# The group norm of an RWKV layer, as a stage of its own or inside the trips of the scan

## The reference, cut to what matters

```python
    _, y = lax.scan(step, S0, (tm(r_h), tm(w_h), tm(k_h), tm(v_h), tm(kk), tm(a_h)))
    y = tm(y)
    mean = jnp.mean(y, axis=-1, keepdims=True)
    var = jnp.mean(jnp.square(y - mean), axis=-1, keepdims=True)
    y = ((y - mean) * lax.rsqrt(var + RW_GN_EPS) * ln_w.reshape(RW_HEADS, RW_HEAD)
         + ln_b.reshape(RW_HEADS, RW_HEAD))
    y = y + jnp.sum(r_h * k_h * r_k, axis=-1, keepdims=True) * v_h
    y = y.reshape(B, T, D) * gate
    return y.astype(h.dtype) @ w_out
```

## Time and profile before

| | us |
|---|---|
| median of three runs | 3041.53 |
| the profiled execution, its own time | 3047.19 |
| span of its trace | 3045.4 |
| scan, from its first DMA issue to the last state update | 514.2 to 955.5 |
| gn, from its first instruction to the next stage's first | 956.5 to 1045.0 |
| PE busy over the span | 2654.7 (87%) |
| DVE, ACT, POOL busy over the span | 884.6, 548.9, 218.2 |
| granted TensorE clock, mean | 0.945 of 2.4 GHz |

### The profile page before, as it was taken

How to read it: one execution, slowest core, us unless ns; L and a number is a source line. 1 busy time by engine, 2 the same in 40 slices (tenths; PEclk the granted TensorE clock), 3 DMA queues, 4 the chain that set the end, 5 groups by cost and what they waited for, 6 DMA issues and landing times. The chain is left out here.

```text
span 3045.4 us, 44485 instructions
## 1 busy us (share of the span) xinstructions
PE 2654.7 (87%) x18608; PEld 1421.0 (47%) x18608; DVE 884.6 (29%) x1598; ACT 548.9 (18%) x892; POOL 218.2 (7%) x209
## 2 busy tenths in 40 slices
PE   5798996989887695999999969999669869999993
PEld 2243442888885253444443434444544534444441
DVE  6233001666565534111110122000762431101013
ACT  3342000223233311000000011300451100000000
POOL 0000000001010400001010000000010010100100
PEclk9999998999998897999999989999889979999997
DMA  3242133131323523799999940221433259999995
GB/s 117 112 143 99 62 103 97 45 82 48 82 49 151 212 118 140 259 413 410 411 407 399 392 152 38 94 79 55 118 130 136 95 196 377 417 413 417 413 404 225
DMA packets 264767, 617.51 MB, mean 203 GB/s; under 512 B 37377, under 2 KB 128658, under 8 KB 262546
## 3 DMA queue, kind: packets, MB, share of 16 engines
q1 hardware_dynamic: 233362, 524.72, 46.3%
q10 hardware_dynamic: 17408, 56.63, 4.7%
q0 software_dynamic: 13824, 33.58, 2.8%
HBM read 545.67 MB, written 85.98 MB: 207 GB/s over the span
## 5 line engine op out<-in xcount | busy, mean ns | idle before, releaser
L1812 PE MATMUL moe_first_psum<-moe_ring,moe_first_x_t 128*64 128x512 f32 (+1 forms) x1504 | 508.9, 599 | 7.3 <-DMA moe_ring<-in_moe_w_in 3.7
L560 PE MATMUL proj_psum<-proj_mix,proj_ring 128*128 128x512 f32 x768 | 337.1, 599 | 15.9 <-ACTq L72 10.1
L1812 PEld LDWEIGHTS moe_first_psum<-moe_ring,moe_first_x_t 128*64 128x64 f32 (+1 forms) x1504 | 198.1, 165 | 280.0 <-issue 275.2
L1812 PE MATMUL moe_first_psum<-moe_ring,moe_first_act_t 128*128 128x512 f32 (+1 forms) x800 | 282.1, 594 | 0.0
L1408 PE MATMUL moe_route_psum<-moe_ring,trunk_mixed 128*128 128x512 f32 x512 | 230.3, 605 | 22.8 <-PEq L106 22.8
L560 PEld LDWEIGHTS proj_psum<-proj_mix,proj_ring 128*128 128x128 f32 x768 | 147.1, 193 | 200.4 <-issue 188.7
L1853 DVE TENSOR_TENSOR moe_first_act<-moe_first_silu,moe_first_psum 128x512 f32<-128x512 f32 x48 | 33.0, 688 | 688.6 <-ACT moe_first_silu L1869 688.6
L2146 PE MATMUL hproj_psum<-trunk_mixed,moe_ring 128*128 128x512 f32 x512 | 220.0, 592 | 1.8 <-ACTq L72 1.8
L1812 PE MATMUL moe_first_psum<-trunk_mixed,moe_first_x_t 128*128 128x512 f32 (+1 forms) x544 | 196.1, 593 | 0.0
L1812 PEld LDWEIGHTS moe_first_psum<-moe_ring,moe_first_act_t 128*128 128x128 f32 (+1 forms) x800 | 105.8, 162 | 131.5 <-issue 131.5
L1408 PEld LDWEIGHTS moe_route_psum<-moe_ring,trunk_mixed 128*128 128x128 f32 x512 | 96.9, 194 | 137.2 <-issue 137.2
(11 more groups left out here) (339 smaller groups left out, 3075.2 us busy)
## 6 DMA issues: line engine op xcount, KB each, us to landing
moe_ring<-in_moe_w_in SPq DMA_DIRECT2D x94, 2048.0 KB, 18.0
moe_ring<-in_moe_w_out SPq DMA_DIRECT2D x50, 2048.0 KB, 19.9
trunk_mixed<-in_moe_w_in SPq DMA_DIRECT2D x34, 2048.0 KB, 20.3
trunk_mixed<-in_moe_w_out SPq DMA_DIRECT2D x14, 2048.0 KB, 21.1
moe_ring<-expert_rows SPq DMA_DIRECT2D x16, 1024.0 KB, 7.9
proj_ring<-in_rw_in SPq DMA_DIRECT2D x12, 1024.0 KB, 6.1
moe_ring<-gate_cm SPq DMA_DIRECT2D x16, 512.0 KB, 4.4
normed_rows<-moe_x SPq DMA_DIRECT2D x16, 512.0 KB, 2.6
```

Of the source, the lines that this page charges most:

```text
L560: mm = pe.matmul(psum[:, bank + half, :], ring[slot][:, k, part * P:(part + 1) * P], src[:, k, half * HALF:(half + 1) * HALF], start=(k == ...
L1812: mm = t.matmul(e.psum[rows, bank + a, :], left[:, k0 + k, rows], weights.units[m % RING][:, k, a * HALF:(a + 1) * HALF], start=(part != " ...
```

## The change

1. **Means, in proj.** Where DVE copied the turned v tile, it now sums each head (a reduce of 1024 columns to 16) and writes v minus the mean as `v_rows`. `v_cm`, read for the bonus, stays as it was. y comes out of the scan with mean zero.
2. **Norm of the trip before, in the scan.** `GroupNorm` (new) works on a tile of 128 tokens, all channels. In trip t ACT squares y of trip t-1 at the start of b = 0; PE sums the squares after step 1 (two products of 512 columns); ACT takes logarithms after step 2 and the inverse root after step 3; POOL multiplies (four pieces of 256 columns); ACT applies weight and bias at the start of b = 1 (eight of 128 columns); POOL adds the bonus and multiplies by the gate (eight pieces).
3. **Bonus of this trip.** POOL multiplies r and k from the tiles that the scan holds (four pieces); PE sums them over heads with eight matrices `rk_ones` after step 1 of b = 1 (eight products of 128 columns); DVE multiplies v with the sums after step 3 of b = 1 (two of 512 columns, and eight small ones before the scan to make `rk_ones`).
4. **Loads.** SP loads a v tile and a gate tile per trip (512 KB each) and, at the start of the scan, the 4 MB of `w_out`. r and k are not loaded again.
5. **Loops.** `all_trips` is written out on every engine.
6. **The last tile's norm goes into moe0_route**: ACT squares, PE sums ahead of the first product, ACT inverts, POOL multiplies behind its tables, ACT applies weight and bias after the first tile's scaling, POOL finishes; PE waits for that ahead of its eighth tile. SP waits for it ahead of loading unit 5, whose memory the norm uses.
7. **The stage gn is gone.** Three units of the weight ring (`late`) live through the whole trunk so that the norm and `w_out` have a place; in the HGRN2 scan three tiles move into it. The routing and mixture code is otherwise the same.

```diff
@@ rwkv_project, vector
-                    v.tensor_copy(mix[0][:, b, :], psum[:, 4 + 2 * b:6 + 2 * b, :].rearrange("p a t -> p (a t)")
-                                  ).then_inc(v_dve.sem, 1)
+                    v.wait_ge(v_dve.sem, v_dve.after("copy", tile - 1))
+                    rows_p = psum[:, 4 + 2 * b:6 + 2 * b, :].rearrange("p a (n e) -> p (a n) e", e=HEAD)
+                    v.tensor_reduce(head_total[:], rows_p, AX_X, ALU.add).then_inc(v_dve.sem, 1)
...
+                    v.scalar_tensor_tensor(out=mix[0][:, b, :].rearrange("p (n e) -> p n e", e=HEAD),
+                                           in0=spread(head_total[:], 2, HEAD), scalar=-1.0 / HEAD, in1=rows_p,
+                                           op0=ALU.mult, op1=ALU.add).then_inc(v_dve.sem, 1)
@@ GroupNorm
+    def sums(self, t, c, source, banks):
+        for half in range(NH):
+            mm = t.matmul(banks[half].rearrange("p (m t) -> p m t", t=P), c.head_ones[:],
+                          source[:, half * (PAIRS // 2):(half + 1) * (PAIRS // 2), :], start=True, stop=True)
+        return mm
+    def bonus_sums(self, t, weights, source, banks):
+        for m in range(PAIRS):
+            at = banks[m // (PAIRS // 2)].rearrange("p (m t) -> p m t", t=P)[:, m % (PAIRS // 2), :]
+            mm = t.matmul(at, weights[:, m, :], source[:, m, :], start=True, stop=True)
+        return mm
+    def unit(self, g, y, tile):
+        for at, pairs in self.pieces(y, tile):
+            ins = g.tensor_tensor(at, at, self.inverse[:, pairs, :], ALU.mult)
+        return ins
+    def affine(self, a, c, y, tile, done):
+        for m in range(PAIRS):
+            at = y[:, m, tile * P:(tile + 1) * P]
+            a.activation(at, at, ACT.Identity, scale=c.col("ln_w")[:, m:m + 1],
+                         bias=c.col("ln_b")[:, m:m + 1]).then_inc(done, 1)
+    def finish(self, g, y, tile, added, finished):
+        for n, (at, pairs) in enumerate(self.pieces(y, tile)):
+            g.tensor_tensor(at, at, self.bonus[:, pairs, :], ALU.add).then_inc(added, 1)
+        g.wait_ge(added, PAIRS // 2 * (tile + 1))
+        for n, (at, pairs) in enumerate(self.pieces(y, tile)):
+            ins = g.tensor_tensor(at, at, self.gate[:, pairs, :], ALU.mult)
+        ins.then_inc(finished, 1)
@@ rwkv_scan
-            with engine.Fori(0, CHUNKS // 2 - 1) as trip:
-                body(trip, False)
-            body(CHUNKS // 2 - 1, True)
+            for trip in range(CHUNKS // 2):
+                body(trip, trip == CHUNKS // 2 - 1)
@@ sync
+            load_tile("v", 0, gn.value, value_in)
+            load_tile("gate", 0, gn.gate, gate_in)
+            outw.load(sp)
...
+                sp.wait_ge(rk_made, trip + 1)
                 load_fresh(trip + 1)
+                sp.wait_ge(pe.sem, pe.after("S.1", trip * 2))
+                load_v(trip * 2 + 2, 0)
+                sp.wait_ge(bonus_made, 2 * trip + 2)
+                load_tile("v", trip + 1, gn.value, value_in)
+                if trip:
+                    sp.wait_ge(finished, trip)
+                    load_tile("gate", trip, gn.gate, gate_in)
+                sp.wait_ge(pe.sem, pe.after("S.1", trip * 2 + 1))
+                load_v(trip * 2 + 3, 1)
@@ gpsimd
                 decayed(trip, 1)
+                bonus_terms(trip)
+                if trip:
+                    g.wait_ge(rooted, trip)
+                    gn.unit(g, y, trip - 1).then_inc(united, 1)
+                    g.wait_ge(shifted, PAIRS * trip)
+                    g.wait_ge(bonus_made, 2 * trip)
+                    g.wait_ge(gate_in, 16 * trip)
+                    gn.finish(g, y, trip - 1, bonus_added, finished)
                 if not last:
                     decayed(trip + 1, 0)
@@ vector
+                        if j == 3 and b == 1:
+                            bonus(trip)
@@ scalar
+                    if b == 0 and trip:
+                        a.wait_ge(act.sem, act.after("Y", chunk - 1))
...
+                        gn.square(a, y, trip - 1).then_inc(squared, 1)
+                    if b == 1 and trip:
+                        a.wait_ge(united, trip)
+                        gn.affine(a, c, y, trip - 1, shifted)
@@ tensor
+                        if j == 1 and b == 0 and trip:
+                            t.wait_ge(mask.sem, mask.after("R.1", chunk))
+                            t.wait_ge(squared, trip)
+                            gn.sums(t, c, gn.inverse, sum_banks).then_inc(summed, 1)
+                        if j == 1 and b == 1:
+                            t.wait_ge(mask.sem, mask.after("R.1", chunk))
+                            t.wait_ge(rk_made, trip + 1)
...
+                            gn.bonus_sums(t, rk_ones, rk, sum_banks).then_inc(bonus_summed, 1)
@@ out_route
+            if gn is not None:
+                t.wait_ge(gn_squared, 1)
+                gn.sums(t, c, gn.inverse, gn_banks).then_inc(gn_summed, 1)
...
+                    if i == TT - 1 and a == 0 and gn is not None:
+                        t.wait_ge(gn_finished, 1)
```

More of the change, by code:

```diff
@@ L807, in _ @@
                 load_v(b, b)
-            with sp.Fori(0, CHUNKS // 2 - 1) as trip:
+            load_tile("v", 0, gn.value, value_in)
+            load_tile("gate", 0, gn.gate, gate_in)
+            outw.load(sp)
+            for trip in range(CHUNKS // 2 - 1):
                 sp.wait_ge(v_trip.sem, v_trip.after("total", trip))
@@ L1105, in body @@
                     read(b, r_b)
+                    if b == 0 and trip:
+                        t.wait_ge(logged, 2 * trip)
+                    if b == 1:
+                        t.wait_ge(bonus_made, 2 * trip + 2)
                     for h in range(2):
@@ L1441, in _ @@
         def _(a):
+            if gn is not None:
+                gn.square(a, u, TT - 1).then_inc(gn_squared, 1)
+                a.wait_ge(gn_summed, 1)
+                for a_half in range(NH):
+                    gn.log(a, c, gn_banks, a_half).then_inc(gn_logged, 1)
+                a.wait_ge(gn_logged, NH)
+                gn.root(a).then_inc(gn_rooted, 1)
             for i in range(TT):
@@ L1997, in combine @@
     with Stage(nc, name) as s:
-        rows = [room.pair[0][:, 2 * b:2 * b + 2, :] for b in range(4)]
+        rows = [room.low_pair[:, 2 * b:2 * b + 2, :] for b in range(4)]
         rows_in = [s.sem(f"rows_in{b}") for b in range(4)]
@@ L2068, in hgrn_project @@
     with Stage(nc, "hproj") as s:
-        rows = [room.pair[3][:, 2 * b:2 * b + 2, :] for b in range(4)]
+        rows = [room.high_pair[:, 2 * b:2 * b + 2, :] for b in range(4)]
         squares = room.units[5][:, 0, :]
@@ L2515, in hgrn_output @@
     with Stage(nc, "hnorm") as s:
-        gate, squares, inv = ([room.pair[0][:, 2 * n + b, :] for b in range(2)] for n in range(3))
+        gate, squares, inv = ([room.low_pair[:, 2 * n + b, :] for b in range(2)] for n in range(3))
         psum = s.psum()
```

242 lines of the change are left out of this document (108 added, 134 removed).

## The result

The changed kernel takes 2996.07 us (median of 4 runs, 2993.91 to 3002.22) against 3041.96 for the kernel before (4 runs, 3041.08 to 3046.58): ratio 0.9849, 95% interval 0.9832 to 0.9867, 45.9 us less. The forecast was 2994, or 47.9 less. A second measurement of the same pair gave 0.9866 (0.9841 to 0.9891). The total came out as predicted; the sum behind it did not. The scan cost 11 us less than forecast, and what lies behind gn, which the prediction took as unchanged but for the route, gave 9 back: 11 us longer mixtures, less some 3 us elsewhere. I use two traces of each kernel: the spans are 3045.4 and 3048.8 before, 3000.2 and 2993.9 after.

The account below looks back on a forecast made before the run. The prediction took the scan as bound by PE and stage gn as 88.6 us that nothing overlaps. Terms of +40.7 against -88.6 gave -47.9 us, or 2994 us from the median of 3041.5; range leaving out 2 in 10: 2973 to 3017.

Parts of the forecast that it names:

- gn: Norm stage between two barriers, overlapped by no other stage: removing it takes 88.6 us off the end.
- Squares' sums: PE, b = 0 chunks, seven trips: two products, four records of 0.43 us, nothing hides them; 12.0 us.
- Bonus sums on PE: b = 1 chunks, eight trips: 1.7 us each, 0.77 covered by a wait for DVE in seven; 8.2 us.
- Bonus on DVE: b = 1, ahead of step 4's additions: two operations delay DVE and so PE by 0.6 us per trip; 4.8 us.
- POOL against DVE: Start of b = 0: one POOL piece per trip lengthens a DVE operation by 0.6 us; 4.8 us.
- DMA: Scan: v and gate loads hold up PE's instructions, 3.5 us over seven trips; queued loads at its start, 3 us.
- ACT and loops: Scan: ACT's new work fits between its copies, 0 us; written-out loops 0, a gain up to 5 us not excluded.
- proj: Projection stage: the last v tile pays one more reduce plus a wait, +1.4 us.
- Route: moe0_route, ahead of PE's first product: square 1.06, a signal 0.2, two products 1.72; +3.0 us.
- Rival A: Scan: only PE's own work is paid, 24.6 us with proj and Route; 2977 us (2971 to 2981), chance 0.17.

Follow-up runs that it names:

- bonus_late: The changed kernel with DVE's bonus products moved from the ladder's step 3 to behind its copies of U: 3002.41 us, ratio 0.9867.
- pool_tiny: The changed kernel with POOL's sixteen pieces per trip on one column each instead of 256, read only up to the scan's end: scan 463.1 us.
- before_loops: The kernel before with only the scan's trips written out on all engines: 3041.04 us, ratio 0.9994.
- before_split: The kernel before with only the weight ring split in two tensors, the HGRN2 scan using the late one: 3047.21 us, ratio 1.0012.
- eps_inside: The changed kernel with the constant gn_eps in a spare column of norm_cols instead of its own tensor: 2987.78 us, ratio 0.9830.
- paced_eps: The changed kernel with the trip's five tile loads spread out of PE's dense stretch and gn_eps in a spare column of norm_cols: 2972.85 us, ratio 0.9770.

## Why the prediction was right, and where its sum was not

- **gn, -88.6:** right. It was the right first row to read: two barriers round one stage.
- **Squares' sums, 12.0:** 7 x 2.04 = 14.3. The 4 x 0.43 is exact; the changeover was not in it. The earlier trace rows couldn't show that, since all their products have 128 rows.
- **Bonus sums on PE, 8.2:** 8 x 2.08 = 16.6, less the wait for DVE that they cover. PE's waits for the other engines fall by 1.05 us per b = 1 chunk, seven times: 7.4 (the prediction had 0.77 of it, the wait for L909 alone; one for L912 goes too). It gives 9.3. The price was 3 us too low and the cover 2 us too small.
- **Bonus on DVE, 4.8:** 0.2 us per trip at most, 1.6 in all (bonus_late). The step that failed: "0.62 us late on DVE is 0.62 late for PE" was read off one pair of chunks and carried to a place with waits of 0.18 and 0.51 us; PE's own work was the longer chain.
- **POOL against DVE, 4.8:** 0 (pool_tiny). The meeting happened, and it met slack. DVE loses 0.4 us at the copy of 16 columns and 0.16 on average at L890's successor, in place of my 0.6; none of it reaches PE. The size was roughly right and the path wrong.
- **DMA, 3.5 and 3.0:** 0 and 0. PE's waits for issue didn't rise, and the first chunk ends 45.3 and 44.5 us after the first load before, 44.4 and 45.2 after. The new burst comes in the ladder, where PE takes some 30 products per us, not in the dense start where it takes 75. That a burst starves PE of instructions is right and costs more than I made it, but it was already paid for before.
- **ACT and loops, 0:** right. PE's waits for ACT's `scan_kb_rows` are 3.8 us before and 3.9 and 4.3 after; the loops are before_loops.
- **proj, +1.4:** the scan's first load is 2.0 later on average; ten kernels with the new copy scatter from 514.2 to 518.2.
- **Route, +3.0:** the pieces are there, square and sums, at the half clock 1.6 longer than counted. Even so gn and route together give -87.0, against -85.6 forecast: some 3 us come back elsewhere between the scan's end and the first mixture, and no run shows where.
- **Missing:** the mixtures. The prediction took all behind the route as unchanged. They give back 3.6 and 7.7 us. By the packets' times, 156.4 to 159.0 ns, my estimate for the 96 units of a mixture, at about 5 us each, is 8 us, of which the constant is 5 and the split 3; that fits the second mixture. In the first, less of it reaches the end.

Scan: forecast +36.3, measured +24.9; 14.3 and 9.3 of it are the two kinds of sums. Behind it 7.7 came back in the last part. Rival A, the cheap scan (20.2 us in the scan), was the better account of the scan; the rest of the program took its gain away. That the total came out 2 us from the forecast is therefore luck: an error of 11 us on one side and of 9 on the other.

What stays open: why the kernels with the same addresses (before_split, eps_inside, paced_eps) spread from 799 to 804 us in the last part. The clock may have a share: in that part it is granted at half for 112.5 us in eps_inside and 126.4 in paced_eps (799.1 and 802.7 us), and for 119.9 and 126.8 in the two traces before (798.8 and 803.2); but before_loops has 126.5 and 799.0. That the alignment is the cause rests on three layouts, in each of which the units that were moved are the slower ones; no run moved one unit alone.

## What to carry to other kernels

When work moves into a saturated queue, price it by the distance to the next start including a changeover of shape, and price its side effects by the slack at the exact spot: a lock shorter than the slack is free, one longer is paid in full (0.58 against 2.21 us here). A burst hurts where the bound engine eats instructions fastest; spread loads over the stretch where it doesn't. The packets of the instruction queue show it: count the instructions that the engine runs between two of them. After any change of layout, compare the stages that were not touched, and look at the start addresses of what big transfers write: here one constant cost between 4 and 8 of the 46 us that the change gained.

## What the runs showed of the hardware that was not expected

- Going over from 64-row to 128-row products of other weights and back cost PE 0.3 us beside the records (2.04 and 2.08 us for a first set, 1.72 and 1.79 for a second).
- Behind a burst of 2.6 MB PE's instructions run out when the DMA engines are idle again (1.88 us up to 790.2, share 0.00 to 0.04): the 16 KB instruction packets, of some 260 instructions, start so far apart that PE runs 384 and 318 between them. A standstill of that kind was followed by 3.4 us at the granted clock 0.50.
- The start of a tile in SBUF changes the time of its 4 KB packets: 159.1 ns where it is a multiple of 256 bytes, 161.6 to 163.1 where it is 32, 96 or 128 bytes off. Over a mixture bound by its weights that is some 8 us when no unit is aligned instead of six of eight.
- A copy of 0.18 us on DVE lasts until the end of the POOL operation that it meets: 0.58 us beside 256 columns, 2.21 beside 1024.
